# Narrow experts of a mixture-of-experts layer: gate and up weights as two groups of 64 stationary columns, with moving widths of 128 down to 88

## What is computed

```
logits = (xf @ router_w + router_b); top_val, top_idx = lax.top_k(logits, 4)
gates = jax.nn.softmax(top_val, axis=-1)
# for the rows xb of one expert e
gu = xb @ w_gu[e] + b_gu[e]              # 1024 -> 2048
gate, up = jnp.split(gu, 2, axis=-1)
gate = jnp.minimum(gate, 7.0); up = jnp.clip(up, -7.0, 7.0)
y = ((up + 1.0) * (gate * sigmoid(1.702 * gate))) @ w_down[e] + b_down[e]
# out[row] += y * gate weight of that row
```

## Time and profile before

| | |
|---|---|
| three runs | 2328.21, 2329.13, 2330.58 us; median 2329.13 |
| profiled execution | 2327.12 us, of which the span of the core is 2325.5 us |
| mean granted TensorE clock | 0.989 |
| PE busy | 2261.4 us (97%) |
| PEld busy | 1898.0 us (82%) |
| DVE, ACT, POOL busy | 751.5, 374.1, 587.9 us |
| DMA | 506.07 MB, mean 218 GB/s |

### The profile page before, as it was taken

One profiled execution on the slowest core, in us unless ns is written; L12 is line 12 of the kernel. 1 busy time (PEld: TensorE's weight loads), 2 busy tenths in 40 slices (PEclk: granted clock), 3 DMA queues, 4 the chain that ended last, 5 costly groups with the idle time before them and its releaser, 6 DMA issues.

```text
span 2325.5 us, 36694 instructions
## 1 busy us (share of the span) xinstructions
PE 2261.4 (97%) x14520; PEld 1898.0 (82%) x14521; DVE 751.5 (32%) x1759; ACT 374.1 (16%) x845; POOL 587.9 (25%) x808
## 2 busy tenths in 40 slices
PE   8999998999987999999999999999999999999997
PEld 5664447768757999999999999998878878878876
DVE  2134776545541162222222222222222222222224
ACT  2222553323320001001111111110000000000002
POOL 1132222232232122222222222322222222222222
PEclk9999999999998999999999999999999999999999
DMA  7000213011119666777788888899999999999996
GB/s 260 1 1 19 29 35 142 28 46 37 56 37 305 220 215 217 227 228 244 254 262 270 278 270 283 283 296 317 332 323 338 321 326 337 324 328 336 324 327 229
DMA packets 377669, 506.07 MB, mean 218 GB/s; under 512 B 14887, under 2 KB 290795, under 8 KB 377448
## 3 DMA queue, kind: packets, MB, share of 16 engines
q1 hardware_dynamic: 362632, 459.56, 59.3%
q0 software_dynamic: 14864, 44.14, 7.2%
HBM read 472.17 MB, written 34.14 MB: 218 GB/s over the span
## 4 chain that ended last, share of the span: by engine, by line
PE 69%; DMA 0%; DVE 0%; issue 0%; POOL 0%; POOLq 0%; DVEq 0%
PE ps L1757 44%; PE ps L1784 12%; PE ps L1769 10%; PE ps L1736 2%; PE ps L1745 1%; DMA arena<-h_dram,arena 0%; DVE arena L1902 0%; DVE arena L2009 0%; POOL out L1636 0%; DVE arena L2015 0%; DVE arena L1995 0%; POOL small L226 0%; DVE small L223 0%; DVEq L2012 0%; POOLq L1636 0%
## 5 line engine op out<-in xcount | busy, mean ns | idle before, releaser
L1757 PEld LDWEIGHTS ps<-arena 128*128 128x128 f32 x8192 | 1029.6, 190 | 8.8 <-issue 7.7
L1757 PE MATMUL ps<-arena 128*128 128x128 f32 (+15 forms) x8192 | 1035.8, 288 | 0.8 <-DVE arena L1902 0.8
L1926 DVE TENSOR_SCALAR arena<-ps,arena 128x128 f32<-128x128 f32 (+15 forms) x256 | 94.6, 370 | 1109.9 <-PE ps L1757 1109.1
L1596 POOL TENSOR_TENSOR arena<-arena 128x128 f32<-128x128 f32 (+15 forms) x256 | 132.0, 516 | 878.0 <-DVEq L1933 878.0
L1668 ACT ACTIVATE arena<-arena 128x128 f32<-128x128 f32 (+15 forms) x256 | 83.3, 325 | 1212.5 <-DVE arena L1926 1212.5
L1784 PE MATMUL ps<-arena 128*128 128x224 f32 (+14 forms) x1920 | 272.4, 303 | 0.0
L1784 PEld LDWEIGHTS ps<-arena 128*128 128x128 f32 x1920 | 270.1, 189 | 0.2
L1769 PE MATMUL ps<-arena 128*128 128x512 f32 x544 | 236.3, 592 | 0.0
L1769 PEld LDWEIGHTS ps<-arena 128*128 128x128 f32 x544 | 102.0, 190 | 122.0 <-issue 121.7
L530 PE MATMUL ps<-arena 128*128 128x384 f32 (+1 forms) x512 | 171.7, 494 | 2.1 <-DVE arena L633 2.1
L530 PEld LDWEIGHTS ps<-arena 128*128 128x128 f32 x512 | 97.5, 193 | 68.3 <-issue 2.7
(11 more groups left out here) (274 smaller groups left out, 1617.2 us busy)
## 6 DMA issues: line engine op xcount, KB each, us to landing
arena<-in_exp_w_gu SPq DMA_DIRECT2D x256, 1024.0 KB, 7.7
arena<-in_exp_w_down SPq DMA_DIRECT2D x64, 2048.0 KB, 9.2
arena<-in_exp_b_down SPq DMA_DIRECT2D x17, 512.0 KB, 10.8
arena<-in_x SPq DMA_DIRECT2D x16, 512.0 KB, 9.0
arena<-in_w_in SPq DMA_DIRECT2D x8, 1024.0 KB, 9.6
h_dram<-arena SPq DMA_DIRECT2D x16, 512.0 KB, 2.7
arena<-in_w_out SPq DMA_DIRECT2D x1, 4096.0 KB, 13.9
arena<-h_dram SPq DMA_DIRECT2D x8, 512.0 KB, 6.9
```

Source lines behind the costliest of these rows:

```text
L1596: v.tensor_tensor(gmn[m % 2][:, 0:n], gmn[m % 2][:, 0:n], umn[m % 2][:, 0:n], ALU.mult).then_inc(S("gum", m % 2), 1)
L1757: last = t_.matmul(bank(m % 4)[:, q * CAP:q * CAP + n], wslot[g][:, k, 256 * q + c:256 * q + c + P], xT[:, k, 0:n], start=(k == 0), stop=( ...
L1926: v.tensor_scalar(gmn[r][:, 0:n], bank(m % 4)[:, 0:n], of[:, m:m + 1], LIMIT, ALU.add, ALU.min).then_inc(S("gmn", r), 1)
```

## The change

`WIDTHS` keeps its first 15 entries; the 17 narrow ranks get widths of their own, from 128 down to 88. In `gate_up`, a rank of at most 128 rows issues two matmuls for each step k in place of one: the first with stationary columns 0 to 63, into partitions 0 to 63 of the bank, the second with columns 64 to 127, into partitions 64 to 127. Elementwise work and the scatter use the new widths too; the gather still fetches 128 rows, and `down_rows` still takes 128 stationary columns. `ORDER` is the identity, so the ranks stay in their order; the bookkeeping (`wide_to`, `narrow_to`, `ROWS`) is written so that another order could be given, and SP's loop over the wide ranks is unrolled.

```diff
-WIDTHS = (224, 204, 196, 184, 176, 168, 164, 160, 156, 152, 148, 144, 140, 136, 132) + (128,) * 17
-TILES = tuple(-(-w // P) for w in WIDTHS)
+WIDTHS = (224, 204, 196, 184, 176, 168, 164, 160, 156, 152, 148, 144, 140, 136, 132,
+          128, 126, 124, 122, 120, 118, 118, 116, 114, 110, 108, 108, 106, 104, 102, 98, 88)
+ORDER = tuple(range(NE))
+ROWS = tuple(WIDTHS[r] for r in ORDER)
+TILES = tuple(-(-w // P) for w in ROWS)
...
-            v.tensor_scalar(by_rank, iota_e[0:NE, :], own, part, ALU.is_equal, ALU.mult).then_inc(S("order"), 1)
+            v.tensor_scalar(by_rank, rank_at[0:NE, :], own, part, ALU.is_equal, ALU.mult).then_inc(S("order"), 1)
...
-            with sp.Fori(0, WIDE) as r:
-                e = sp.value_load(tab[0:1, ds(r + T_MAIN, 1)], min_val=0, max_val=NE - 1)
-                weights(e, r)
-            for r in range(WIDE, NE):
+            for r in range(NE):
                 e = main_expert(sp, r)
                 weights(e, r)
...
-                    scatter(idx[r % 3], r, WIDTHS[r])
+                    scatter(idx[r % 3], r, ROWS[r])
...
                         for k in range(KT):
-                            last = t_.matmul(bank(m % 4)[:, q * CAP:q * CAP + n], wslot[g][:, k, 256 * q + c:256 * q + c + P],
-                                             xT[:, k, 0:n], start=(k == 0), stop=(k == KT - 1))
+                            for c0, c1 in (((0, P),) if n > P else ((0, P // 2), (P // 2, P))):
+                                last = t_.matmul(bank(m % 4)[c0:c1, q * CAP:q * CAP + n],
+                                                 wslot[g][:, k, 256 * q + c + c0:256 * q + c + c1],
+                                                 xT[:, k, 0:n], start=(k == 0), stop=(k == KT - 1))
...
-                gate_up(r, WIDTHS[r], lambda m: rows_out_main(r - 1, m))
+                gate_up(r, ROWS[r], lambda m: rows_out_main(r - 1, m))
```

More of the change, by code:

```diff
@@ L27 @@
 CAP = 256
-WIDTHS = (224, 204, 196, 184, 176, 168, 164, 160, 156, 152, 148, 144, 140, 136, 132) + (128,) * 17
-TILES = tuple(-(-w // P) for w in WIDTHS)
+WIDTHS = (224, 204, 196, 184, 176, 168, 164, 160, 156, 152, 148, 144, 140, 136, 132,
[3 more added lines that the diff above has]
+TILES = tuple(-(-w // P) for w in ROWS)
 WIDE = sum(n == 2 for n in TILES)
-assert len(WIDTHS) == NE and max(WIDTHS) <= CAP and all(n == 2 for n in TILES[:WIDE])
+assert len(WIDTHS) == NE and max(WIDTHS) <= CAP and sorted(ORDER) == list(range(NE))
 NMORE = SEQ * TOPK // CAP + NE
@@ L45 @@
 C_WIDTH = C_IOTA + NE
-C_BLK = C_WIDTH + NE
+C_RANK = C_WIDTH + NE
+C_BLK = C_RANK + NE
 C_HALF, C_EPS = C_BLK + NMORE, C_BLK + NMORE + 1
@@ L76, in program @@
         iota_b = cst[:, C_BLK:C_BLK + NMORE]
+        rank_at = cst[:, C_RANK:C_RANK + NE]
         def level(l):
@@ L1482, in program @@
         LAST = NE - 1
-        assert TILES[LAST] == 1 and LAST > WIDE
+        assert TILES[0] == 2 and TILES[LAST - 1] == TILES[LAST] == 1
         def more_expert(eng, i):
@@ L1496, in wide_to, with narrow_to @@
         def wide_to(r):
-            return min(r, WIDE)
+            return sum(n == 2 for n in TILES[:r])
+        def narrow_to(r):
+            return r - wide_to(r)
         ffn = ExitStack()
@@ L1519, in weights @@
                                  ).then_inc(S("w_in0", g), 16)
-            with sp.Fori(0, WIDE) as r:
-                e = sp.value_load(tab[0:1, ds(r + T_MAIN, 1)], min_val=0, max_val=NE - 1)
-                weights(e, r)
-            for r in range(WIDE, NE):
+            for r in range(NE):
                 e = main_expert(sp, r)
                 weights(e, r)
[L1527 to L1530, removed]
+                if TILES[r] == 1:
+                    q = narrow_to(r)
+                    if q >= 2:
+                        sp.wait_ge(S("bd_used"), q - 1)
+                    sp.dma_start(bd_row[q % 2], exp_b_down[0, ds(e, 1), :].rearrange("o n -> (o n)").partition_broadcast(P)
+                                 ).then_inc(S("bd_in", q % 2), 16)
             def load_h(t):
@@ L1622, in _ @@
                     pool.wait_ge(S("y_out"), 16 * tiles_to(r - 1))
-                    scatter(idx[(r - 1) % 3], r - 1, WIDTHS[r - 1])
-                gated(r, WIDTHS[r], (lambda m: scatter_main(r - 1, m)) if r < LAST else (lambda m: tile_roots(0, 0) if m == 5 else None))
+                    scatter(idx[(r - 1) % 3], r - 1, ROWS[r - 1])
+                gated(r, ROWS[r], (lambda m: scatter_main(r - 1, m)) if r < LAST else (lambda m: tile_roots(0, 0) if m == 5 else None))
             last_rows = idx[LAST % 3]
@@ L1644, in last_sums @@
                     pool.wait_ge(S("hc_in", t), 16)
-                scatter(last_rows, LAST, WIDTHS[LAST])
+                scatter(last_rows, LAST, ROWS[LAST])
                 pool.wait_ge(S("y_out"), 16 * TALL)
@@ L1788, in rows_out_main @@
             def rows_out_main(r, m):
-                if r >= WIDE:
+                if r < 0 or TILES[r] == 1:
                     return
-                if r >= 0 and m == 3:
-                    pe.wait_ge(S("yv"), 8 * r + 8)
+                if m == 3:
+                    pe.wait_ge(S("yv"), 8 * wide_to(r) + 8)
                     rows_out(0, r, tiles_to(r))
-                if r >= 0 and m == 4 and TILES[r] == 2:
+                if m == 4:
                     rows_out(1, r, tiles_to(r))
@@ L1799, in _ @@
                 pe.wait_ge(S("xT_sb"), 2 * tiles_to(r + 1))
-                gate_up(r, WIDTHS[r], lambda m: rows_out_main(r - 1, m))
+                gate_up(r, ROWS[r], lambda m: rows_out_main(r - 1, m))
                 if r + 1 < NE:
                     rows_in(r + 1, tiles_to(r + 1), wide_to(r + 1), TILES[r + 1])
-                if r < WIDE:
-                    down(r, WIDTHS[r], tiles_to(r), r)
+                if TILES[r] == 2:
+                    down(r, ROWS[r], tiles_to(r), wide_to(r))
                 else:
@@ L1941, in rows_out_narrow @@
                     dve.wait_ge(S("yt_ps", q), tiles_to(r + 1))
-                    v.tensor_tensor(half, bank(6 + q), bd_row[r % 2][:, 512 * q:512 * (q + 1)], ALU.add).then_inc(S("tr_bank", q), 1)
+                    v.tensor_tensor(half, bank(6 + q), bd_row[b % 2][:, 512 * q:512 * (q + 1)], ALU.add).then_inc(S("tr_bank", q), 1)
                 dve.drain()
@@ L1947, in rows_out_main @@
             def rows_out_main(r, m):
-                if r >= WIDE:
+                if r < 0:
+                    return
+                if TILES[r] == 1:
                     if m == 3 and r + 1 < LAST:
@@ L1955, in rows_out_main @@
                     rows_out(0, tiles_to(r), rec[r % 3])
-                if r >= 0 and m == 4:
-                    if TILES[r] == 2:
-                        rows_out(1, tiles_to(r), rec[r % 3])
+                if m == 4:
+                    rows_out(1, tiles_to(r), rec[r % 3])
                     dve.drain()
@@ L2002, in _ @@
             dve.wait_ge(S("hg_in"), 16)
-            dve.wait_ge(S("bd_in", LAST % 2), 16 * ((LAST - WIDE) // 2 + 1))
-            v.scalar_tensor_tensor(hg, bd_row[LAST % 2], gate, hg, ALU.mult, ALU.add)
+            b_last = narrow_to(LAST)
+            dve.wait_ge(S("bd_in", b_last % 2), 16 * (b_last // 2 + 1))
+            v.scalar_tensor_tensor(hg, bd_row[b_last % 2], gate, hg, ALU.mult, ALU.add)
             dve.drain()
```

14 lines of the change are left out of this document (8 added, 6 removed).

## The result

The changed kernel is slower: a median of 2347.16 us (2346.5 to 2349.09, four runs) against 2329.86 us, ratio 1.0076 with a 95% interval of 1.0059 to 1.0094. The forecast was 2281 us in a range of 2272 to 2300. It is 66 us off: a gain of 48 us was expected, and a loss of 17 came. TensorE does run the new passes a little faster than forecast, and then it waits.

A forecast was written before the change was run, and what follows sets the result against it. It took TensorE, busy for 97% of the span, as the bound: 56.7 us from columns less 5.5 for switches and 3 at the end gives 48.2, so 2278.9 from 2327.1, predicted as a 2281 us median, range 2272 to 2300.

The forecast's parts named there:

- Elementwise work and scatter get narrower, nothing waits for them: Narrow ranks: DVE and POOL are busy 10.34 and 10.73 of 43 us and still fit at 35; no cost charged.
- The chain is TensorE's, the pass costs N/1.2 + 5, a 128-column load is the floor: Gate and up matmuls: TensorE time sets the total; a pass takes 111.6 ns, and loading 128 stationary columns costs about as much.
- Two groups overlap: Gate and up matmuls: passes and loads of the two 64-column halves run beside each other, a pair costing N/1.2 + 5 ns.
- the lower bound, N/1.2 + 3: Least price of a pair in ns, since a stream cannot go faster than its columns; 9 us better in all.
- Rival 2: Gate and up pairs cost more than N/1.2 + 5, as halves hold each other up: 17 us at +9, 2298; chance 0.08.
- Switches cost 5.5 us: TensorE passing between 128 and 64 stationary columns and back in narrow ranks: 19 x 0.29 us, on the path.
- 266 columns give 56.7 us: Gate and up matmuls of the 17 narrow ranks: 266 fewer moving columns, 256 x 266/1.2 ns gained.
- The weights' lead pays for the shortfall: Weight loads: at 360 GB/s ranks from 108 to 98 fall 5.8 us short; a 28 us lead covers it, no wait.
- rival 1: The weights bind: at only 330 GB/s, 16 to 19 us of shortfall remain, 2299 us; chance 0.10.
- The end gives back 3 us: Last rank and final norm: TensorE finishes sooner but the norm follows other clocks, so 3 us of the gain are lost.
- The bound of 6: Upper end of the 1 to 6 us of gain expected to be given back at the last rank.
- Rivals 3 to 5: Halves' weight loads take turns (2356 us, 0.05), their matmuls take turns (2707, 0.03), or a rank overflows its width (2380, 0.02).

The follow-up runs named there:

- the fifth kernel: The kernel before, with scatters from the second narrow rank on at 122 rows in place of 128: 2477.86 us, ratio 1.0636.
- the sixth: The kernel before, with scatters from the second narrow rank on at 120 rows in place of 128: 2329.77 us, ratio 1.0.
- the eighth: The changed kernel in its old order, with narrow widths that divide well (126 down to 88) and scatters as wide as the ranks: 2286.41 us, ratio 0.9816.
- the ninth: The changed kernel with wide and narrow ranks by fours, widths that divide well and scatters as wide as the ranks: 2273.7 us, ratio 0.9757.
- experiment 4: The changed kernel with one group of 128 stationary columns in place of two of 64, and scatters of 128 rows: 2329.73 us, ratio 1.0001.
- experiment 1: The changed kernel, but each narrow rank scatters 128 rows again: 2291.24 us, ratio 0.9828 to the kernel before.
- The seventh kernel: The changed kernel with scatters of 128 rows and wide and narrow ranks by fours, ranks of 120 to 128 columns last: 2277.31 us, ratio 0.9773.
- experiment 3: The kernel before with only the narrow ranks' scatter rows following the changed list of widths: 2343.09 us, ratio 1.0061.

## Why the prediction was wrong

**The step that failed** is the one that put the scatter at nothing: "Elementwise work and scatter get narrower, nothing waits for them". Both halves of that sentence were unfounded. It counted rows, and what a scatter costs here is over how many DMA engines they go. And something does wait for it: POOL ahead of the next list, and the weight transfers of SP. The views do not show single engines; that the weights wait for their share on the engines that are behind is my reading of the drop to 26 GB/s.

The software queue's packets give the rule. Suppose that N rows are spread over k engines, k the largest divisor of N up to 16, and that each engine left out gets as many small packets as a busy one has rows. Then a scatter has (16 - k) x N/k small packets and 128 - N rows fewer than before. For the 16 ranks that are scattered with the list 128 to 98, k is 16, 14, 4, 2, 15, 2, 2, 4, 6, 11, 12, 12, 2, 13, 6, 14. This sums to 4514 small packets less 226 rows = 4288, and the page has 19152 - 14864 = 4288. The 4514 are also the difference in packets under 512 bytes above. For 15 scatters of 122 rows the rule gives 15 x (854 - 6) = 12720, and the fifth kernel has 27584, which is 12720 more; for 120 rows 8 - 8 = 0, and the sixth has 14864; for the list of the eighth, 96, and it has 14960; for the ninth, whose order scatters a rank of 88 columns (k = 11) in place of one of 126, 80, and it has 14944. All five agree to the packet. That the busy share in the gap is between one and two tenths fits 2 of 16 engines; which engines they are, no run here shows.

The landing times go by k too, and not by the number of rows. The scatters of the changed kernel from 124 to 102 rows, each by itself:

| rows | 124 | 122 | 120 | 118 | 118 | 116 | 114 | 110 | 108 | 108 | 106 | 104 | 102 |
|---|---|---|---|---|---|---|---|---|---|---|---|---|---|
| k | 4 | 2 | 15 | 2 | 2 | 4 | 6 | 11 | 12 | 12 | 2 | 13 | 6 |
| lands after, us | 17.2 | 30.0 | 9.2 | 29.1 | 28.9 | 17.0 | 14.5 | 11.3 | 10.1 | 9.6 | 26.6 | 9.1 | 13.3 |

The Trainium skill states the rule for k (DMA: Bandwidth & Descriptors, Why a DMA increments its semaphore by 16 and not by 1): the number of engines is the largest up to 16 that divides the slowest dimension of both sides. The traces agree, by the packets and the landing times above. The small packets are my addition, from the counts. I did not weigh it against the scatter ahead of the prediction, where it would have named the ranks of 122, 118, 118 and 106 columns.

Point by point:
- *The chain is TensorE's, the pass costs N/1.2 + 5, a 128-column load is the floor*: right. Widths without the split changed nothing (experiment 4).
- *Two groups overlap*, read from one burst of 32-column passes: right, also for 64 columns and 128 moving. A pair costs N/1.2 + 3.1, not + 5, which makes it 256 x 17 x 1.9 ns = 8 us cheaper in all. The price measured lies at the lower bound, N/1.2 + 3; no row stood behind the 3 of that bound, so that it fits is luck. Rival 2, dearer pairs, is out.
- *Switches cost 5.5 us*: consistent, not isolated. Split and switches together came out 3.8 us faster; with 8 us from the pairs that leaves about 4 for the switches, of which the 0.16 us a rank at the transposes are 2.7. By the chain alone the gain would be 5.6, so this difference is good to some 2 us.
- *266 columns give 56.7 us*: right by the chain, where 256 pairs take 27.67 us at 126 columns and 25.96 at 118 (experiment 1), 0.83 ns a column. From the split alone at 2325.9 it would be 2269 us with nothing else in the way. No kernel reached its full sum: the ninth, with 281 columns (59.9 us), would be at 2266 and is at 2273.7; 5.5 us of the difference are idle time of TensorE in its narrow ranks.
- *The weights' lead pays for the shortfall*: wrong in size, and rival 1 was nearer. I priced the flow at 360 GB/s; with no pause it was 343 to 358 (experiment 1). At 350 a rank needs 14.2 MB / 350 = 40.6 us, and by the measured price of a pair a rank takes 256 x (N/1.2 + 3.1) ns + 14.8 us: 40.3 at 116, 39.0 at 110, 36.5 at 98. Nine ranks in place of six fall short, by 0.3 to 4.1 us each and 19 us together in place of 5.8. The lead still covers most of that, but then the loads for the last rank are late, and with them what comes behind.
- *The end gives back 3 us*: mis-sized. With the padded scatter it gave back 15: 50.5 us from the start of the last rank to the end of L2006, against the 35.1 worked out. The bound of 6 left out that the h tiles queue behind the last weights: their first square began 27.5 us after the rank's start, not 18.7. The squares hold up what POOL multiplies, and TensorE waits 6.7 us for that in L1778 (experiment 1's page). The seventh kernel undoes it by order alone.
- *Rivals 3 to 5*: no sign of them.

In numbers: TensorE's own sum is 2269 us. The weights' shortfall and the end bring it to 2291 (experiment 1), and the scatters on few engines to 2347. The prediction charged 3 us where the first two took 22, and nothing for the scatters, which took 56.

How the 56 us divide can be read from the two profiled executions, whose spans are 53.9 us apart: TensorE is idle for 43 us more, and busy for 10.8 us more (2220.3 against 2209.5) with the same passes. The three longest waits for weights ahead of the last rank, from TensorE's timeline:

```profile
1887.71 16.17 PE L1765 MATMUL ps<-arena 128*64 128x116 f32 x288 [4.76 <-DMA arena<-in_exp_w_gu]
1935.61 15.95 PE L1765 MATMUL ps<-arena 128*64 128x114 f32 x288 [11.71 <-DMA arena<-in_exp_w_gu]
2190.98 14.91 PE L1765 MATMUL ps<-arena 128*64 128x102 f32 x288 [9.08 <-DMA arena<-in_exp_w_gu]
```

Each wait ends within 1 us of the landing of a scatter with k = 2: of 118 rows, issued at 1857.94 and at 1906.08 and landed at 1887.0 and 1935.0, and of 106 rows, issued at 2163.45 and landed at 2190.1. From 1930 to 1940, around the end of the 11.71 us, the granted clock is 0.54; such stretches are where extra busy time comes from. The first scatter of 122 rows costs no wait for weights: the lead absorbs it, and 2.36 us for DVE at 1812 are all that TensorE is idle. After it every stretch of 50 us up to the end has idle time, so the scatter of 106 rows, absorbed in experiment 3, costs 9.08 us here. The chain leaves TensorE at 1708, for POOL's products and then the scatter of 124 rows (k = 4), issued at 1730.89.

## What to carry to other kernels

Before a DMA's number of rows is changed, factor it: 120 and 122 rows differ by 148 us here, and an indirect DMA padded to 128 rows is cheaper than an exact one whose number of rows has no large divisor up to 16. Of a queue on which other transfers depend, ask not how much it carries but over how many engines, and who waits for it. When TensorE gets faster in one part of a kernel, add up the bytes of that part, price them at the rate that flows without a pause, and put the parts that compute faster than they load between those that compute more slowly, above all not at the end.

## What the runs showed of the hardware that was not expected

- A scatter with a small k holds up the weight transfers of another queue: some 26 GB/s in place of 350 for about 11 us in a scatter of 122 rows, landing after 29.1 us in place of 8.6 with 120 rows.
- Two groups of 64 stationary columns by turns are slightly cheaper than one of 128 at the same 128 moving columns: 109.8 ns against 111.6, the switch in included.
- A wait of TensorE costs more than itself: after 9.70 us idle its clock was at 0.50, and the passes behind took 216 ns in place of 111.6 until it rose (experiment 5). 41 of the 149 us between the spans of that run and of the kernel before are longer busy time.
- The DMA share in these pages passes 1.0 where nothing pauses (1.07 at 343 to 358 GB/s). A share of 1.00 at 328 GB/s was thus not the ceiling, as the prediction says, but only 4 to 8% below the steady flow.
